# Two transformer-like blocks on one core: the prologue's order of loads, squares and shift columns

## What is computed

```python
def rmsnorm(x, g):
    y = xf * lax.rsqrt(jnp.mean(xf * xf, axis=-1, keepdims=True) + EPS)
    return (y * g)
def modulated_norm(x, g, shift, scale):
    return rmsnorm(x, g) * (1.0 + scale[:, None, :]) + shift[:, None, :]

def short_conv_layer(x, c, mod_w, mod_b, norm_g, w_in, conv_w, w_out):
    shift, scale, gate = modulation(c, mod_w, mod_b, 3)   # silu(c) @ mod_w + mod_b, split
    h = modulated_norm(x, norm_g, shift, scale)
    proj = h @ w_in                                       # 1024 x 4096
    b_gate, c_gate, u, z = jnp.split(proj, 4, axis=-1)
    y = b_gate * causal_dwconv(c_gate * u, conv_w)
    y = y * jax.nn.silu(z)
    return x + gate[:, None, :] * (y @ w_out)
```

## Time and profile before

| | |
|---|---|
| median of three runs | 2774.36 us |
| profiled execution | 2773.0 us |
| its span | 2771.2 us |
| TensorE busy | 2678.9 us (97%) |
| VectorE busy | 1724.0 us (62%) |
| ScalarE busy | 1227.2 us (44%) |
| GpSimd busy | 1204.5 us (43%) |
| granted clock, mean | 0.99 |

### The profile page before, as it was taken

How to read it: one execution, slowest core, us unless ns; L and a number is a source line. 1 busy time by engine, 2 the same in 40 slices (tenths; PEclk the granted TensorE clock), 3 DMA queues, 4 the chain that set the end, 5 groups by cost and what they waited for, 6 DMA issues and landing times.

```text
span 2771.2 us, 38861 instructions
## 1 busy us (share of the span) xinstructions
PE 2678.9 (97%) x13088; PEld 2129.9 (77%) x13088; DVE 1724.0 (62%) x2246; ACT 1227.2 (44%) x1855; POOL 1204.5 (43%) x823
## 2 busy tenths in 40 slices
PE   6999999999999998999999999999999999989998
PEld 4888887887777776888877777777788888868886
DVE  7867667336767866591025555555445777688888
ACT  4423324224545554442246776675335433334442
POOL 1378522223555553222221121111123988858886
PEclk9999999999999999999999999999999999999999
DMA  5132432574112112113320010012433344374442
GB/s 231 61 107 99 156 140 76 190 239 155 54 48 82 53 71 104 53 60 111 125 92 31 34 39 31 31 37 70 159 145 114 141 154 156 121 262 160 167 159 91
DMA packets 104422, 305.34 MB, mean 110 GB/s; under 512 B 10112, under 2 KB 10752, under 8 KB 103296
## 3 DMA queue, kind: packets, MB, share of 16 engines
q1 hardware_dynamic: 104320, 304.05, 30.4%
HBM read 227.46 MB, written 76.55 MB: 110 GB/s over the span
## 4 chain that ended last, share of the span: by engine, by line
PE 71%; issue 17%; DVE 5%; ACT 3%; POOL 2%; DMA 1%; SPq 0%; POOLq 0%; DVEq 0%; ACTq 0%
PE PS L936 27%; PE PS L1461 11%; PE PS L1513 9%; PE PS L1040 7%; PE PS L1207 5%; PE PS L1179 2%; PE PS L1112 2%; POOL WL L3119 2%; PE PS L1141 2%; PE PS L1156 2%; PE PS L1365 2%; PE PS L1346 1%; DVE dM L3051 1%; PE PS L1305 1%; DVE dM L3092 1%
## 5 line engine op out<-in xcount | busy, mean ns | idle before, releaser
L3119 POOL TENSOR_TENSOR WL<-WR,WH 128x1024 fp32r<-128x1024 f32 x123 | 307.9, 2503 | 1163.5 <-ACT WH L1552 1056.2
L936 PE MATMUL PS<-HH,WH 128*128 128x512 f32 x1392 | 445.7, 401 | 17.1 <-POOL WL L3119 5.7
L936 PE MATMUL PS<-HL,WH 128*128 128x512 f32 x1392 | 432.8, 392 | 0.0
L936 PE MATMUL PS<-HH,WL 128*128 128x512 f32 x1392 | 431.4, 391 | 0.0
L936 PEld LDWEIGHTS PS<-HH,WH 128*128 128x128 f32 x1392 | 255.0, 189 | 79.5 <-issue 22.6
L936 PEld LDWEIGHTS PS<-HH,WL 128*128 128x128 f32 x1392 | 263.0, 189 | 56.6
L936 PEld LDWEIGHTS PS<-HL,WH 128*128 128x128 f32 x1392 | 263.0, 189 | 56.3
L3183 POOL TENSOR_TENSOR bB<-bB,bC 128x256 f32<-128x256 f32 (+7 forms) x128 | 189.9, 1493 | 191.2 <-DVE bC L2668 191.2
L2668 DVE TENSOR_TENSOR_SCAN bC<-bN,EPSC 128x256 f32<-128x256 f32 (+7 forms) x128 | 222.3, 1747 | 57.6 <-ACT bN L1832 53.1
L1552 ACT ACTIVATE WH<-WR 128x1024 fp32r<-128x1024 f32 x123 | 130.4, 1060 | 198.9 <-PE PS L936 116.6
L3051 DVE TENSOR_TENSOR dM<-PS,dM 128x512 f32<-128x512 f32 x212 | 137.9, 682 | 10.6 <-PE PS L1513 9.6
(11 more groups left out here) (397 smaller groups left out, 6447.7 us busy)
## 6 DMA issues: line engine op xcount, KB each, us to landing
WR<-wst SPq DMA_DIRECT2D x125, 512.0 KB, 3.5
uRAW<-wst SPq DMA_DIRECT2D x32, 512.0 KB, 4.7
hid<-uT SPq DMA_DIRECT2D x32, 512.0 KB, 2.8
dRAW<-wst SPq DMA_DIRECT2D x64, 256.0 KB, 3.3
HLF<-hid SPq DMA_DIRECT2D x28, 512.0 KB, 8.6
GLF<-hid SPq DMA_DIRECT2D x28, 512.0 KB, 7.9
aRAW<-wst SPq DMA_DIRECT2D x24, 512.0 KB, 4.2
MR_KV<-mods SPq DMA_DIRECT2D x24, 512.0 KB, 4.9
```

What stands on the lines that cost most here:

```text
L936: last = pe.matmul(PS[:, dst0 + q:dst0 + q + HALF], l, rr[:, k * S + q:k * S + q + HALF], start=a, stop=z)
L3119: pool.tensor_tensor(WL[slot][:, :], WR0[:, :], WH[slot][:, :].bitcast(F32), ALU.subtract).then_inc(w_lo, 1)
```

## The change

The prologue is put in another order, and four chunks instead of two are made from X that isn't normalised.

- Loads: the constants come first, the first weight tile goes to WR0, then each part of X with its two scale rows; the second weight tile is loaded directly into the room of WL[1] and replaced there by its low part. Weight tiles 2 and 3 are loaded behind the last scale row into the temporaries T[3] and T[0], the eight shift rows behind these. Tile 4 is loaded once AE[0] is made.
- VectorE makes only coefficients and HL per k. The additions of the squares and the shift rows follow. The squares lie in the second half of MRAW, where the scale rows were.
- TensorE starts with chunks 0 and 1. Chunks 2 and 3 follow in PSUM pairs 2 and 3 with weights WHX and WLX. The squares are summed into pair 0 behind k = 2 of these, once ScalarE has copied chunk 0 to WR0. Shift columns are fp32r products with two columns (high and low part of the shift, tile SHR), in two blocks.
- The root goes to a tile of its own, ARS. Chunks 0 to 3 leave as AE[0] to AE[3]. Chunks 4 and 5 are interleaved, 6 and 7 follow.
- The mixes 2 and 3 move from the first column tile's outputs to the second's.

The diff, cut to its core:

```diff
@@ SyncE
+            sp.dma_start(IDF[:, :], consts[:, K_ID:K_ID + P]).then_inc(ld_c, 16)
+            sp.dma_start(TRF[:, :], consts[:, K_TRI:K_TRI + P]).then_inc(ld_c, 16)
             for g in range(4):
+                if g == 0:
+                    sp.dma_start(WR0[:, :], wst[0]).then_inc(ld_w, 16)
                 sp.dma_start(X[:, 2 * g * S:2 * (g + 1) * S], xt[:, 2 * g * S:2 * (g + 1) * S]).then_inc(ld_x[g], 16)
+                for k in (2 * g, 2 * g + 1):
+                    load_row(k, KT + k)
+                    if k == 0:
+                        sp.dma_start(WL1F[:, :], wst[1]).then_inc(ld_w1, 16)
+            sp.wait_ge(s_sc, 1)
+            sp.wait_ge(ld_w, 16)
+            sp.dma_start(WLXF[0], wst[2]).then_inc(ld_w, 16)
+            sp.wait_ge(ld_w1, 16)
+            sp.dma_start(WLXF[1], wst[3]).then_inc(ld_w1, 16)
             for k in range(KT):
-                for m in (k, KT + k):
-                    sp.dma_start(MRAW[:, m * D:(m + 1) * D], mods[m]).then_inc(ld_k[k], 16)
+                sp.wait_ge(ld_k[k], 16)
+                load_row(k, k)
+            sp.wait_ge(a_ready, A_DONE)
             sp.dma_start(WR0[:, :], wst[4]).then_inc(ld_w, 16)
@@ TensorE
+            for k in range(KT):
+                pe.wait_ge(a_raw_lo, k + 1)
+                step(C_AIN, 0, 0, HH, HL, k)
+                step(C_AIN + 1, 1, 1, HH, HL, k)
+            for k in range(KT):
+                if k == 3:
+                    squares_of_x()
+                if k == 6:
+                    pe.wait_ge(a_ready, KT + 2)
+                    pe.wait_ge(free[1], u[1] + 1)
+                    shift_columns(0)
+                    shift_columns(1).then_inc(a_raw_read, 1)
+                early_step(0, k)
+                last = early_step(1, k)
+                if k < KT - 1:
+                    last.then_inc(a_raw_read, 1)
+            shift_columns(2)
+            shift_columns(3).then_inc(a_raw_read, 1)
+            pe.wait_ge(rs, 1)
+            for k in range(KT):
+                pe.wait_ge(f_lo, FILL["a"] + (k + 1))
+                step(4, 0, 0, HH, HL, k)
+                if k == 3:
+                    pe.wait_ge(a_shift, 5)
+                if k >= 3:
+                    step(5, 1, 1, HH, HL, k - 3)
+            for k in range(KT - 3, KT):
+                step(5, 1, 1, HH, HL, k)
@@ ScalarE
             for k in range(KT):
                 act.wait_ge(ld_x[k // 2], 16)
+                act.wait_ge(a_ready, k + 1)
+                act.activation(kt(HH, k), kt(X, k), ACT.Identity, scale=col(COEF, k)).then_inc(a_raw_hi, 1)
+                if k == 0:
+                    act.wait_ge(ld_w1, 16)
+                    act.activation(WH[1][:, :], WL1F[:, :], ACT.Identity).then_inc(w_hi, 1)
                 ins = act.activation(kt(XSQ, k), kt(X, k), ACT.Square)
...
+            act.wait_ge(chunk_done, C_AIN + 2)
+            act.activation(WR0[:, :], PAIR[0], ACT.Identity).then_inc(free[0], 1)
+            act.wait_ge(ss, 1)
+            root(ARS[:, :], PAIR[0], ARST[:, :])
             def first_input(k):
+                act.wait_ge(a_raw_read, k + 1 if k < 6 else KT) if k < KT - 1 else act.wait_ge(chunk_done, C_AIN + 5)
+                if k == 5:
+                    split_w(4, 0)
+                if k == 6:
+                    act.wait_ge(a_raw_read, KT + 1)
...
             fill_hi("a", 0, before=first_input)
+            split_w(5, 1)
@@ VectorE
+            scale(0)
             for k in range(1, KT):
-                shift_and_scale(k)
+                scale(k)
                 raw_low(k - 1)
             raw_low(KT - 1)
+            for k in range(0, KT, 2):
+                dve.wait_ge(sq, k + 1)
+                dve.tensor_tensor(kt(XSQ, k), kt(XSQ, k), kt(XSQ, k + 1), ALU.add).then_inc(sq_pair, 1)
+            for k in range(KT):
+                dve.wait_ge(ld_k[k], 32)
+                modulation(col(MOD, k), kt(MRAW, k))
...
+            dve.wait_ge(rs, 1)
+            dve.wait_ge(free[0], 2)
+            dve.tensor_tensor(AE[0][:, :], WR0[:, :], ARS[:, :], ALU.mult).then_inc(a_ready, 1)
...
+            early_out(1).then_inc(free[1], 1)
             def first_input(k):
+                if k == 6:
+                    links(early_out(2))
+                    links(early_out(3))
```

More of the change, by code:

```diff
@@ new lines, in _, with early_step, shift_columns @@
+            u = USED["ain"]
+            def early_step(m, k):
+                b = slice(k * P, (k + 1) * P)
+                if k == 0:
+                    pe.wait_ge(w_hi, C_AIN + 3 + m)
+                    pe.wait_ge(w_lo, C_AIN + 3 + m)
+                last = mm3((2 + m) * S, WHX[m][:, b], WLX[m][:, b], HH, HL, k, k == 0, k == KT - 1)
+                if k == KT - 1:
+                    last.then_inc(chunk_done, 1)
+                return last
+            def shift_columns(m):
+                hi, lo = ((WH[0], WL[0]), (WH[1], WL[1]), (WHX[0], WLX[0]), (WHX[1], WLX[1]))[m]
+                for k in range(KT):
+                    for half in (hi, lo):
+                        last = pe.matmul(PS[:, S + 2 * m:S + 2 * m + 2], half[:, k * P:(k + 1) * P],
+                                         SHR[:, 2 * k:2 * k + 2], start=k == 0 and half is hi,
+                                         stop=k == KT - 1 and half is lo)
+                return last
@@ new lines, in squares_of_x @@
+            def squares_of_x():
+                pe.wait_ge(free[0], u[0] + 1)
+                for k in range(0, KT, 2):
+                    pe.wait_ge(sq_pair, k // 2 + 1)
+                    for h in (0, HALF):
+                        last = pe.matmul(PS[:, h:h + HALF], ONES[:, :], kt(XSQ, k)[:, h:h + HALF],
+                                         start=k == 0, stop=k == KT - 2)
+                        last.then_inc(ss if h and k == KT - 2 else sq_added, 1)
+            pe.wait_ge(free[0], u[0])
@@ new lines, in _ @@
+            shift_columns(2)
[10 more added lines that the diff above has]
+                step(5, 1, 1, HH, HL, k)
+            for n in range(2, 4):
+                chunk(4 + n, n % 2, n % 2, u[n % 2] + 2)
@@ L1042, in block_pair @@
                     last.then_inc(sa_p, 1)
-            input_chunks(0, first=True)
-            for j in range(1, A_FIRST):
-                input_chunks(j)
             block_pair(0, 0, first=True)
@@ L2300, in fill_lo @@
                             dve.wait_ge(f_lo, FILL[name] + k - 1)
-                        mul_mul(kt(X, k) if name == "a" else T[2 + k % 2], kt(X, k), scale(k), T[0]).then_inc(ftmp, 1)
+                        if name == "a":
+                            mul_mul(kt(X, k), kt(X, k), scale(k), ARS[:, :]).then_inc(ftmp, 1)
+                        else:
+                            mul_mul(T[2 + k % 2], kt(X, k), scale(k), T[0]).then_inc(ftmp, 1)
                     if k:
```

227 lines of the change are left out of this document (99 added, 128 removed).

## The result

The changed kernel is slower: 2785.12 us median (2781.88 to 2788.21, 5 runs) against 2774.36 (2771.97 to 2774.73, 5 runs), ratio 1.0043, 95% interval 1.0028 to 1.0057. That is 11.9 us (7.8 to 15.8), outside my range of 2764.5 to 2779. The profiled execution took 2785.12, its span is 2783.2.

A forecast was written before the change was run, and what follows sets the result against it. TensorE was taken as the bound, through when it begins line 1040's block products: 10.0 us earlier start, less 6.9 squares, 1.4 wait and 0.8 clock, with 0.9 of joints gone, gives 1.8 off: 2772.5 us, range 2764.5 to 2779.

The forecast's parts named there:

- The step that failed: From the block products of line 1040 to the end: any shift in their start was carried straight to the end.
- Start: TensorE's first chunk matmul: forecast at 18.4 us against 28.44 before, 10.0 earlier, bounds 16.8 and 19.5.
- the stretched HL that was charged: VectorE's first HL beside GpSimd's WL: taken at 3.38 us instead of 1.27, so done at 18.4.
- the half rate behind it: TensorE's first matmuls after the start: half clock was forecast to cost 2.5 us.
- S: The time when the squares in TensorE's stream end: forecast 57.8 us.
- Shift columns: 64 single-pass records in TensorE's prologue: 7.2 us as before, in two blocks of 3.6; bounds 5 and 12.
- The wait: TensorE at chunk 5's k 0 waits for tile 5's WL from 84.0 to 90.2: 6.2 us, bounds 3.5 and 8.5.
- Half rate again: Behind the wait for tile 5, TensorE's clock was forecast to fall to half, costing 3.8 us.
- Sum of the prologue: All prologue terms together: block products begin at 132.1 against 133.93, 1.8 us earlier.
- next stage isn't ready: Rival: waits ahead of chunk 6 and the first block product, plus half rate; 6.1 us slower, 2780.5; chance 0.13.
- 2762.5: Full price of the rival that the cover holds: no wait at tile 5, no clock loss, 11.8 us earlier; chance 0.25.

The follow-up runs named there:

- e1: The changed kernel with SHR in unused bytes, so later tiles keep their old addresses, order of work unchanged: 2768.07 us, ratio 0.9985 to the kernel before.
- e10: e9 with chunk 5's steps begun beside chunk 4's k6 instead of k3: 2771.85 us, ratio 1.0001 to the kernel before.
- e9: e5 with ScalarE copying tile 4's high half one step earlier: 2771.34 us, ratio 0.9999 to the kernel before.
- e5: e1 with the four shift columns spread among full steps instead of two blocks: 2772.74 us, ratio 1.0001 to the kernel before.
- e3: The kernel before with every tile from X on 128 bytes higher: 2771.99 us, ratio 1.0002.
- e4: The kernel before with only the weight tiles 128 bytes higher and everything behind them 256 higher: 2802.52 us, ratio 1.0106.
- e8: The kernel before with only the weight tiles 64 bytes higher and everything behind them 256 higher: 2808.99 us, ratio 1.0126.

## Why the prediction was wrong

**The step that failed** is the first paragraph's: "Behind that point TensorE has no gap and the code is unchanged but for counts, so I carry a shift there straight to the end." The instructions were the same, their operands' addresses were not. The diff has the `place` line in plain view, and I counted SHR's instructions but not what its room does to the tiles behind it: a term that I put at nothing. In its place the runs show about 16 us (e1 against the changed kernel). By address 2712 matmuls with GH, GL, YPH, YPL, MXH or MXL as the moving operand pay newly, and 192 with HH or HL against temporaries, which had paid, no longer do: 2520 net, 13 to 17 us at 5 to 6.7 ns.

The same step is wrong a second time, in a smaller way. Behind the prologue the kernel before does have gaps: TensorE's waits from 140 us on sum to some 57 us in its trace. And a lead isn't carried straight to the end: e1's is 6.3 us at the third block, 5.6 at the first products of line 1003 (455.1 against 460.7), 4.3 at those of line 1261 (650.7 against 655.0) and 3.0 at the last matmul. Which of these waits takes it, no run shows.

**Start.** 18.4 forecast, 18.50 measured, with the stretched HL that was charged. VectorE's and GpSimd's rows ahead of it:

```profile
14.70 3.44 DVE L2426 SCALAR_TENSOR_TENSOR HL<-X,COEF,HH 128x1024 fp32r<-128x1024 f32 x1
```

```profile
14.70 2.35 POOL L3198 TENSOR_TENSOR WL<-WL1F,WH 128x1024 fp32r<-128x1024 f32 x1 [4.14 <-ACT WH L1647]
```

Right, and so are the half rate behind it (matmuls stand 0.425 apart until 22.9) and S: squares from 50.85, forecast 50.8, end 57.9, forecast 57.8. The profile's clock column doesn't show this first half rate; it reads 1.00 in the window where only six matmuls run:

```profile
20.00:22.00 2.00, 2.00 (x6) 1.57 (x5) 1.96 (x4) 1.73 (x2) 0.00 (x0) 1.00 1.02 420
```

Ahead of the first recorded change of the clock the distance of the matmuls tells the rate, the column doesn't.

**Shift columns.** They begin at 66.05 for 66.0 and stand 0.11 apart. Their price was right and their effect was missed: 3.5 us of half rate in the full matmuls behind. The clock fell to 0.50 while the profile has TensorE busy for all of the window (2.00 of 2.00 at 72 to 74), so the profile's busy share doesn't forecast it. The Trainium skill (TensorE: Matmul & The Clock Gate, section Part 1, the HAM clock gate) says the gate follows how busy the engine is; I had applied that to idle time alone.

**The wait.** 6.2 forecast, 0.65 measured. TensorE came 3.5 later, at 87.54, and tile 5 was ready 2.2 sooner, at 88.04. These are the rows of VectorE and GpSimd in the changed kernel that I had priced with the stretch on VectorE:

```profile
75.85 1.28 DVE L2364 SCALAR_TENSOR_TENSOR HL<-X,MOD,HH 128x1024 fp32r<-128x1024 f32 x1
```

```profile
75.82 3.53 POOL L3194 TENSOR_TENSOR WL<-WR,WH 128x1024 fp32r<-128x1024 f32 x1 [36.48 <-ACT WH L1609]
...
85.50 2.54 POOL L3194 TENSOR_TENSOR WL<-WR,WH 128x1024 fp32r<-128x1024 f32 x1 [6.16 <-ACT WH L1609]
```

Of the pair at 75.8 GpSimd was stretched, which held nobody up, and VectorE kept its 1.28; the outputs AE 2 and 3 that follow it read PSUM and ran beside the rest of the split unstretched. So the 2.1 that I charged to VectorE's chain for tile 4's split did not come. In the earlier trace rows it was VectorE, 3.38. The stretch is real, its side isn't fixed: what is added is each time about the other's length (3.44 beside 2.35; 3.53 beside 1.28, where 2.4 is usual), as if one stood until the other was done.

**Half rate again.** 3.8 forecast behind the wait, none came: behind 0.65 the clock stayed at 1.00, as it did behind 1.54 in e10. The mechanism was right in kind and the size too high: behind waits of 5.60 (e9) and 4.04 (e10) 2.2 and 2.7 us were lost. In e5 5.6 were lost behind only 2.43, but there 16 narrow products stand inside the stretch; how much is theirs isn't shown.

**Sum of the prologue.** Line of block products at 132.1 forecast, 126.47 measured: 10.0 charged for wait and clock, 4.2 happened. The rival "next stage isn't ready" came in part: no wait ahead of chunk 6, but 1.55 ahead of the third block, behind GL subtractions that took longer than in the earlier trace rows:

```profile
126.63 6.84 DVE L2334 TENSOR_TENSOR GL<-GLF,GH 128x512 fp32r<-128x512 f32 x4
```

For the prologue alone the forecast of 1.8 us gained lies inside what e1 measured, 4.0 (1.7 to 6.7), and that is in part luck: the 5.6 us too few at the line of block products were made up by 1.55 of a wait ahead of the third block and by what the lead lost on its way to the end. That the whole came out slower has none of my rivals' causes. (My range of 2764.5 to 2779 also left out the full prices of two of them, 2762.5 and 2780.5.)

## What to carry to other kernels

A diff that adds or resizes a tile moves all tiles placed behind it: list the start addresses before and after, and compare moving operand and stationary tile modulo 256 before any step is called unchanged. When a long stretch shows TensorE busy at 100% and full clock, count its matmuls per window; that is where a changed price per matmul shows. Before cover is taken off a wait, work out when the next two tiles are ready, not only the next one, and from what stands ahead of their loads in the queue.

## What the runs showed that I had not expected

- 5 to 6.7 ns on a 128x512 fp32 matmul of about 227 by the relative start of its two operands modulo 256; at a difference of 64 no less than at 128, none when all tiles move together (e3). 30 us over the kernel in e4, 36 in e8.
- Behind each of two blocks of 32 two-column matmuls, 0.11 us apart and without a gap, the granted clock was 0.50; behind blocks of 16 between full matmuls it stayed at 1.00 (e5, e9).
- When GpSimd and VectorE run side by side from SBUF, one of them is stretched, and not always the same one: 3.44 for VectorE beside 2.35 for GpSimd at 14.70, 3.53 for GpSimd beside 1.28 for VectorE at 75.8. Moving a split by one step moved the stretch onto VectorE and cost its chain 2.1 (e9).
